# A routed two-expert decoder step on one core: the first two tiles take their slots from the position counts, and four pieces of the order move

## What is computed

```python
h = x @ w_in                      # 1024 -> 2048: values, two gates, conv input
y = concat(pool_out, conv_out) @ w_out
x = layer_norm(ALPHA * x + y)
# top-1 group of 4, then top-2 of its 8 experts
g_top, g_idx = top_k(softmax(x @ w_group + b_group), 1)
e_top, e_idx = top_k(softmax(e_logits_of_that_group), 2)
gate = g_top * e_top / sum(e_top)
for e in range(32):
    hdn = silu(x @ w1[e]) * (x @ w3[e])     # 1024 -> 512
    acc += combine[:, e] * (hdn @ w2[e])    # 512 -> 1024
out = layer_norm(ALPHA * x + acc)
```

## Time and profile before

| what | value |
|---|---|
| median of 3 runs | 716.95 us (716.07 to 717.56) |
| the profiled execution | 716.73 us |
| its span | 715.0 us |
| PE busy (matmul) | 609.8 us, 85% |
| DVE, ACT, POOL busy | 306.9, 181.8, 158.4 us |
| moved by the DMA queues | 235.99 MB, mean 330 GB/s |
| of it weights of the experts | 96 loads of 2048 KB |

### The profile page before, as it was taken

How to read it: one execution, slowest core, us unless ns; L and a number is a source line. 1 busy time by engine, 2 the same in 40 slices (tenths; PEclk the granted TensorE clock), 3 DMA queues, 4 the chain that set the end, 5 groups by cost and what they waited for, 6 DMA issues and landing times.

```text
span 715.0 us, 10596 instructions
## 1 busy us (share of the span) xinstructions
PE 609.8 (85%) x4220; PEld 420.6 (59%) x4220; DVE 306.9 (43%) x787; ACT 181.8 (25%) x287; POOL 158.4 (22%) x181
## 2 busy tenths in 40 slices
PE   5999999999999999889877987988788777877771
PEld 5999999878775556446444544554344435453440
DVE  4462485517577133353442353342434251433244
ACT  3323313302111313223232323322232121223130
POOL 1000000000000414244235224332341322233142
PEclk9999999999989999999999999899999999999996
DMA  9952133834496999999999999999999999999950
GB/s 250 282 184 90 45 118 105 339 135 190 152 392 250 390 418 420 417 416 417 422 416 421 413 422 416 422 416 421 422 418 421 415 422 420 425 415 418 404 223 21
DMA packets 45738, 235.99 MB, mean 330 GB/s; under 512 B 13667, under 2 KB 18275, under 8 KB 28712
## 3 DMA queue, kind: packets, MB, share of 16 engines
q1 hardware_dynamic: 32287, 220.92, 76.6%
q0 software_dynamic: 12544, 11.71, 4.9%
q10 hardware_dynamic: 857, 2.67, 0.9%
HBM read 237.69 MB, written 30.20 MB: 375 GB/s over the span
## 4 chain that ended last, share of the span: by engine, by line
PE 34%; issue 19%; DMA 17%; SPq 15%; POOL 9%; DVE 5%; ACT 1%; POOLq 0%; DVEq 0%; ACTq 0%
PE ps L534 14%; SPq L402 9%; PE ps L591 7%; DMA tenth_block<-in_w 6%; DMA blocks<-in_w 6%; PE ps L694 6%; SPq L406 5%; PE ps L715 2%; POOL out L1085 2%; POOL out L1081 2%; POOL prev L1077 2%; POOL first_outputs L1073 2%; DMA first_outputs<-ye,first_row 2%; DMA x_tok<-in_x_prompt 1%; DMA prev<-first_outputs,final_row 1%
## 5 line engine op out<-in xcount | busy, mean ns | idle before, releaser
L694 PE MATMUL ps<-blocks,ln 128*64 128x256 f32 x1952 | 233.5, 396 | 53.6 <-DMA blocks<-in_w 32.4
L694 PEld LDWEIGHTS ps<-blocks,ln 128*64 128x64 f32 x1952 | 157.0, 143 | 130.2 <-issue 57.2
L715 PE MATMUL ps<-blocks,hT 128*64 128x512 f32 x464 | 105.7, 596 | 6.0 <-DMA blocks<-in_w 5.8
L1077 POOL DMA_INDIRECT prev<-first_outputs,final_row x32 | 34.9, 1091 | 246.7 <-DMA first_outputs<-ye_more,first_row 119.3
L715 PEld LDWEIGHTS ps<-blocks,hT 128*64 128x64 f32 x464 | 32.8, 137 | 59.8 <-issue 48.5
L798 ACT ACTIVATE ln<-ps 128x512 f32<-128x512 f32 (+1 forms) x38 | 19.9, 572 | 112.2 <-PE ps L682 89.0
L1494 DVE SCALAR_TENSOR_TENSOR h_rows<-silu,slot_gate,ps 128x256 f32<-128x256 f32 x33 | 15.7, 477 | 69.0 <-PE ps L694 68.9
L1499 DVE COPY hT<-ps 128x256 f32<-128x256 f32 x33 | 13.9, 422 | 71.1 <-PE ps L703 71.1
L534 PE MATMUL ps<-xT_high,w_in_high 128*128 128x288 f32 x256 | 41.4, 305 | 0.9 <-DVE xT_low L1187 0.9
L981 ACT ACTIVATE std<-rstd,eps 128x1 f32<-128x1 f32 x32 | 9.4, 295 | 125.3 <-DVEq L1523 125.2
L534 PE MATMUL ps<-xT_low,w_in_high 128*128 128x288 f32 x256 | 39.5, 297 | 0.0
(11 more groups left out here) (232 smaller groups left out, 789.6 us busy)
## 6 DMA issues: line engine op xcount, KB each, us to landing
blocks<-in_w SPq DMA_DIRECT2D x87, 2048.0 KB, 36.5
tenth_block<-in_w SPq DMA_DIRECT2D x9, 2048.0 KB, 37.9
blocks<-in_w_in SPq DMA_DIRECT2D x3, 2048.0 KB, 10.5
blocks<-in_w_out SPq DMA_DIRECT2D x2, 2048.0 KB, 7.8
x_tok<-in_x_prompt SPq DMA_DIRECT2D x4, 512.0 KB, 5.2
blocks<-in_w_in SPq DMA_DIRECT2D x4, 512.0 KB, 11.3
first_outputs<-in_x_prompt SPq DMA_DIRECT2D x4, 512.0 KB, 8.7
x_rows<-x_tok ACTq DMA_DIRECT2D x4, 512.0 KB, 2.7
```

The lines of the kernel that those rows point to most:

```text
L694: mm = pe.matmul(ps[64 * g:64 * g + 64, bank, 0:FH], x, w[:, k, g * FH:(g + 1) * FH], start=(k == 0), stop=(k == KD - 1))
L715: mm = pe.matmul(ps[64 * g:64 * g + 64, BY, :], hT[:, k % 2, k // 2 * SLOTS:(k // 2 + 1) * SLOTS], w[:, k, g * DH:(g + 1) * DH], start=(k ...
L1077: return g.indirect_dma_start(out=prev[w], out_offset=None, in_=first_rows[:, :], in_offset=rows_at(idx), bounds_check=last_row, oob_is_er ...
```

## The change

- **Head.** `project(0)`'s first half no longer waits for the low part of the weights before its first 16 matmuls, only before the last 8; the turn of tile 3 moves behind this first half.
- **Mask.** VectorE makes `mask` from the chosen group and experts directly, before `picked`, and the two differences for the gates behind it. The position and count matmuls take 64 rows instead of 128 for the last tile.
- **Slots of tiles 0 and 1.** `hot_first` comes from two small operations on the position counts of experts 0 and 1 and two comparisons, in place of the matching over all ten choices. It stands before the sums for the table.
- **First pair.** TensorE's order after tile 0's w3 becomes: gather of tile 1, table matmuls, turn of tile 1, tile 1's w1, turn of tile 0's hidden, tile 1's w3, down of tile 0. ScalarE copies tile 1's rows before it waits for the table.
- **End.** The last w2 is loaded in two halves with a semaphore each, and `down` waits for the second one midway. VectorE does `final(31)` before `products(32)`, and the last tile's sum in two parts: the filled row first, the product when it comes; POOL issues `store(31)` ahead of `load(31)`, and `load(31)` ahead of `send(30)`. The stores count on two semaphores by even and odd tile.

The diff, cut to its core (the semaphores' declarations, and the loop for further tiles, which does not run here, are left out):

```diff
@@ -454,7 +455,12 @@
             def load(n):
                 kind, t = LOADS[n]
-                if kind == "w2":
+                if kind == "w2" and t == E:
+                    e = expert_of(t)
+                    src = w2[bass.DynSlice(e, 1)].rearrange("e f d -> (e f) d").rearrange("(g p c) d -> p g c d", g=2, c=KF // 2)
+                    for g, landed in ((0, block_loaded[HOME[n]]), (1, last_loaded)):
+                        sp.dma_start(out_block(HOME[n])[:, 2 * g:2 * g + 2, :], src[:, g, :, :]).then_inc(landed, 16)
+                elif kind == "w2":
                     load_out(HOME[n], expert_of(t))
...
@@ -500,7 +506,7 @@
                     mm.then_inc(x_turned, 1)
 
-            for j in range(4):
+            for j in range(3):
                 turn_x(j)
...
@@ -519,17 +525,20 @@
 
                 part, g = c // NG, c % NG
-                pe.wait_ge(w_low, c + 1)
+                pe.wait_ge(w_high, c + 1)
                 if c in (2, 3) or 4 <= c < 10:
                     pe.wait_ge(in_act, c - 1)
                 elif c >= 10:
                     pe.wait_ge(in_dve, c - 9)
                 for h in range(2):
                     if c == 0 and h:
+                        turn_x(3)
                         turn_x(4)
                     if c == 0:
                         pe.wait_ge(xT_low, (6, 2 * NT)[h])
                     for i, (a, b) in enumerate(((0, 0), (0, 1), (1, 0))):
+                        if a:
+                            pe.wait_ge(w_low, c + 1)
                         for k in range(KD):
...
@@ -703,14 +711,14 @@
                 mm.then_inc(h_turned, 1)
 
-            def down(b, loads, seq, halfway=None):
+            def down(b, loads, seq, last=False):
                 w = out_block(b)
                 pe.wait_ge(block_loaded[b], loads)
                 wait(pe, y_kept, seq)
                 pe.wait_ge(hT_ready, seq + 1)
                 for k in range(KF):
-                    if halfway and k == KF // 2:
-                        halfway()
+                    if last and k == KF // 2:
+                        pe.wait_ge(last_loaded, 16)
                     for g in range(2):
...
@@ -723,13 +731,14 @@
                 into_hidden("w1", 0, 16, 0, 0)
                 into_hidden("w3", 1, 16, 0, 0)
+                fetch_first(1)
                 token_table()
-                fetch_first(1, lambda: turn_hidden(0))
-                down(2, 16, 0, lambda: turn_first(1))
+                turn_first(1)
                 pe.wait_ge(xeT_ready, 2)
                 into_hidden("w1", 3, 16, 1, 1)
+                turn_hidden(0)
                 into_hidden("w3", 4, 16, 1, 1)
-                pe.wait_ge(table_ready, 1)
+                down(2, 16, 0)
                 turn_hidden(1)
...
@@ -751,7 +760,7 @@
                 into_hidden("w3", *place("w3", E), E, 0)
                 turn_hidden(E)
-                down(*place("w2", E), E)
+                down(*place("w2", E), E, last=True)
 
...
@@ -999,11 +1008,11 @@
             keep_xeT_first(0)
             silu_of(0)
-            act.wait_ge(table_ready, 1)
             keep_xe_first(1)
-            fill_second()
             keep_xeT_first(1)
             silu_of(1)
+            act.wait_ge(table_ready, 1)
+            fill_second()
             keep_xeT(1)
...
@@ -1097,11 +1106,12 @@
             def store(t):
                 pool.wait_ge(y_kept, t + 1)
-                store_first(t % YR, first_row[:, t:t + 1]).then_inc(first_stored, 16)
+                store_first(t % YR, first_row[:, t:t + 1]).then_inc(more_first if t == E else first_stored[t % 2], 16)
 
             def load(t):
+
                 w = (t - 1) % ZR
-                pool.wait_ge(first_stored, 16 * t)
+                pool.wait_ge(first_stored[(t - 1) % 2], 16 * ((t - 1) // 2 + 1))
                 wait(pool, final_stored[w], 32 * ((t - 1) // ZR))
...
@@ -1126,12 +1136,17 @@
             store(1)
             load(2)
-            for t in range(2, E):
+            for t in range(2, E - 1):
                 store(t)
                 send(t - 1)
-                load(t + 1)
+                if t < E - 2:
+                    load(t + 1)
                 if t % 2 == 0 and t // 2 + 2 <= PAIRS:
                     fetch(t // 2 + 2)
+            store(E - 1)
+            load(E - 1)
+            send(E - 2)
+            load(E)
             send(E - 1)
...
@@ -1354,7 +1369,6 @@
             gmax, m1, m2, ex = [top[:, i, :] for i in range(4)]
             choose(EG, lg, gmax, g_hot, g_tmp)
-            v.tensor_tensor(g_tmp, lg, gmax.unsqueeze(2).to_broadcast([P, NT, EG]), ALU.subtract).then_inc(diff_ready, 1)
 
...
@@ -1363,6 +1377,11 @@
             settled(v.scalar_tensor_tensor(e_val, e_hot[:, :, 0, :], -3.0e38, e_val, ALU.mult, ALU.add))
             choose(EPG, e_val, m2, e_hot[:, :, 1, :], e_tmp)
+            settled(v.tensor_tensor(e_tmp, e_hot[:, :, 0, :], e_hot[:, :, 1, :], ALU.add))
+            v.tensor_tensor(mask.rearrange("p n (g e) -> p n g e", g=EG),
+                            g_hot.unsqueeze(3).to_broadcast([P, NT, EG, EPG]),
+                            e_tmp.unsqueeze(2).to_broadcast([P, NT, EG, EPG]), ALU.mult).then_inc(mask_ready, 1)
+            v.tensor_tensor(g_tmp, lg, gmax.unsqueeze(2).to_broadcast([P, NT, EG]), ALU.subtract).then_inc(diff_ready, 1)
             v.tensor_tensor(m2, m2, m1, ALU.subtract).then_inc(diff_ready, 1)
...
@@ -1370,8 +1389,6 @@
             settled(last)
             settled(v.memset(picked[64:P, NT - 1, :, :], 0.0))
-            v.tensor_tensor(mask, picked[:, :, 0, :], picked[:, :, 1, :], ALU.add).then_inc(mask_ready, 1)
-
 
...
@@ -1380,42 +1397,22 @@
                 return x.unsqueeze(1).to_broadcast([P, n, x.shape[-1]])
 
+            dve.wait_ge(pos_done, 1)
+            pos_of = ps[:, 5, 0:NT * E].rearrange("p (n e) -> p n e", n=NT)
+            slot_of = first_slot[:, :].rearrange("p (i n) -> p i n", i=2)
+            for i in range(2):
+                last = v.scalar_tensor_tensor(slot_of[:, i, :], pos_of[:, :, i], 1.0, mask[:, :, i], ALU.add, ALU.mult)
+            settled(last)
+            settled(v.tensor_scalar(first_slot[:, :], first_slot[:, :], -1.0, None, ALU.add))
+            for i in range(2):
+                v.tensor_tensor(hot_first[:, i, :, :], iota[:, :].unsqueeze(1).to_broadcast([P, NT, SLOTS]),
+                                slot_of[:, i, :].unsqueeze(2).to_broadcast([P, NT, SLOTS]), ALU.is_equal).then_inc(hot_ready, 1)
+
             settled(v.tensor_tensor(prod, pick, row(iota[:, 0:E], A), ALU.mult))
             settled(v.tensor_reduce(expert, prod, AX.X, ALU.add))
             dve.wait_ge(tail_stored, 64)
-            dve.wait_ge(pos_done, 1)
-            settled(v.tensor_tensor(product, picked, ps[:, 5, 0:NT * E].rearrange("p (n e) -> p n e", n=NT)
-                                    .unsqueeze(2).to_broadcast([P, NT, 2, E]), ALU.mult))
+            settled(v.tensor_tensor(product, picked, pos_of.unsqueeze(2).to_broadcast([P, NT, 2, E]), ALU.mult))
             settled(v.tensor_reduce(pos, prod, AX.X, ALU.add))
-
-            settled(v.tensor_scalar(col, pos, float(SLOTS), 1.0e6, ALU.is_ge, ALU.mult))
-            settled(v.scalar_tensor_tensor(base, expert, float(SLOTS), pos, ALU.mult, ALU.add))
-            settled(v.tensor_tensor(rel[:, :], base, col, ALU.add))
-
-            def match_slots(n):
-
-                wait(dve, hot_ready, n)
-                wait(dve, rel_moved, n)
-                v.tensor_tensor(equal[:, :, :], iota[:, :].unsqueeze(1).to_broadcast([P, A, SLOTS]),
-                                rel[:, :].unsqueeze(2).to_broadcast([P, A, SLOTS]), ALU.is_equal).then_inc(matched, 1)
-
-            both = equal[:, :, :].rearrange("p (n k) c -> p n k c", k=2)
-
-            def sum_choices(n, into):
-                dve.wait_ge(matched, n + 1)
-                v.tensor_tensor(into, both[:, :, 0, :], both[:, :, 1, :], ALU.add).then_inc(hot_ready, 1)
-
-            def move_rel(n):
-
-                dve.wait_ge(matched, n + 1)
-                v.tensor_scalar(rel[:, :], rel[:, :], -float(SLOTS), None, ALU.add).then_inc(rel_moved, 1)
-
-            match_slots(0)
-            move_rel(0)
-            sum_choices(0, hot_first[:, 0, :, :])
-            match_slots(1)
-            sum_choices(1, hot_first[:, 1, :, :])
-
 
...
@@ -1507,10 +1504,13 @@
 
             def finish(t, u, w, in_order):
-
                 dve.wait_ge(y_kept, t + 1)
                 in_order(v.tensor_tensor(prev[w], prev[w], ye[u], ALU.add))
                 dve.sem_inc(prev_added, 1)
+                norm2(t, w, in_order)
+
+            def norm2(t, w, in_order):
+
                 in_order(v.bn_stats(stats[:, 0, :], prev[w]))
...
@@ -1532,6 +1532,18 @@
                     dve.wait_ge(ln2_loaded, 64)
                 finish(t, t % YR, w, settled)
+
+            def last_final():
+
+                u, w = E % YR, (E - 1) % ZR
+                dve.wait_ge(prev_loaded[w], 16 * ((E - 1) // ZR + 1))
```

(14 more changed lines are left out.)

28 lines of the change are left out of this document (14 added, 14 removed).

## The result

| | before | after |
|---|---|---|
| median | 717.25 us (716.07 to 718.53) | 726.44 us (724.48 to 730.07, 4 runs) |
| ratio, 95% interval | | 1.0127 [1.0092, 1.0162] |
| profiled execution, span | 716.73, 715.0 | 724.48, 722.7 |

The changed kernel is 1.3% slower, and the interval is clear of 1. Its profiled execution is the fastest of its four. I compare the two traces first, and come back to the other 2 us of the median at the end.

What follows compares the result with a forecast made beforehand. The DMA queues' stream of expert weights (413 to 425 GB/s from 250 to 661 us) sets the end, not TensorE. Forecast 716.73 - 2.3 (head) + 5.5 (refill, slots included) + 4.7 (end) = 724.6 us, range 718.0 to 729.0.

Steps and rivals of the forecast that it cites:

- Head, -2.3: First products: clock stays up, second half product starts at 18.5 instead of 20.86 us, a gain of 2.3 us.
- the other end that the prediction gave, -0.6: Head: if the clock falls as before, the first half costs 1.7 us more and only -0.6 is left.
- this shift is carried to the release of the early blocks: Head: TensorE works almost without a gap to 160 us, so the -2.3 reaches the early blocks' release.
- Slots, -0.6: Routing: tile 0's gather starts at 208.16 instead of 208.76, behind keep_warm; only 0.6 of some 2.2 us arrives.
- the 64-row matmuls cost and save nothing: Routing: taking 64 rows for the last tile's position and count matmuls changes the time by nothing.
- Refill, +5.5: First pair: load 12 at 243.1 instead of 237.03, queue idle 13.3 instead of 7.8 us; +5.5, slots' 0.6 included.
- the stall before pair 1: Refill: TensorE stands idle for the turn of pair 1, worth nothing while the queue holds three blocks.
- End, +4.7: After the last landing: products(32) waits behind final(31), +2.7, and TensorE's low clock costs 2.0 more.
- Rival A: Stream makes the refill gap up, so late load 12 costs nothing; 714.6 or 717.7 us; chance 0.12.
- Rival B: End pays: load(31) lands before 690.6, two-part sum saves 1.4, total 718.5 us; chance 0.16.
- Rival C: Slow side: head's clock falls (-0.6) and load(31) lands late (+6.5), total 728.1 us; chance 0.12.
- D: Rival that changes don't do what they say; already forecast in the slots, where keep_warm takes most; no chance of its own.

Runs made afterwards that it cites:

- e1: Changed kernel with TensorE's old order of the first pair and tile 0's sum ahead of tile 1's products; 721.44 us.
- e2: Changed kernel with the old end (VectorE's order, one sum, POOL's order, last w2 in one piece); 722.64 us.
- e3: Changed kernel with old first pair and old end, leaving the new head, early mask and slots from counts; 717.69 us, ratio 1.0009.
- e5: Kernel before with the new head alone; 716.14 us, ratio 1.0000.
- e10: e9 with 14 instead of 21 keep_warm matmuls ahead of the position matmuls; 714.53 us, ratio 0.9969.
- e6: Changed kernel with tile 0's hidden turn and down directly behind the turn of tile 1, ahead of tile 1's w1; 725.59 us, ratio 1.0116.
- e8: e3 with the two-part sum and the last w2 in halves kept, products and copy of tile 32 ahead of final(31); 717.49 us, ratio 1.0007.
- e9: e3 with 2 instead of 12 keep_warm matmuls behind the position matmuls; 716.39 us, ratio 0.9992.
- e7: Changed kernel with VectorE's copy of tile 0's hidden turn moved behind the release of the table; 726.92 us, ratio 1.0127.
- e11: Changed kernel with the table matmuls ahead of the gather of tile 1, tile 0's down still last; 728.06 us, ratio 1.0153.
- e4: Kernel before with final(31) moved ahead of products(32) on VectorE, nothing else; 723.02 us, ratio 1.0080.
- e12: e9 with the old head; 716.85 us, ratio 0.9996.

## Why the prediction was right, and where it was off

- **The forecast** was 724.6; the profiled execution took 724.48, the median 726.44. The range (718.0 to 729.0) holds both, and the sign and the two causes are as argued. The closeness of the first is luck: the runs spread over 5.6 us, and two errors cancel. Up to the last `w3` the sum has +3.2 and the traces +2.3; behind it the sum has +4.7 and the traces +5.4.
- **Head, -2.3.** The second half product came at 17.53, a microsecond sooner than the 18.5 given, and then lost it to the clock, whose fall I had looked for in the first half only. At the release -1.8 was left. Where the clock stayed up (e1, e2, e3, e5, e10) the second half starts at 17.9 to 18.3 and -2.4 to -2.6 arrives, as forecast; where it fell in the first half (e6, e8, e9), at 19.4 to 19.7 and -1.1 to -1.5 arrives, toward the other end that the prediction gave, -0.6; in e7 and e11 the half starts later still and nothing arrives. I had taken one of two cases for the rule: the clock stayed up in five of eleven traces of the new head. The step that failed is the next one: "this shift is carried to the release of the early blocks" is true, but the sum went on as if it were carried to the end. In medians the head, mask and slots together, -2.3 - 0.6 by my terms, gave +0.4 (e3, not to be told from 0). Behind the release stands a stretch at 1.2 GHz whose length has two values 3.4 us apart, and I had priced the `keep_warm` there by one trace of the shorter kind.
- **Slots, -0.6.** "Twelve more `keep_warm` matmuls hold TensorE" is right: the gather starts right behind them. But only 0.28 of the 0.6 arrived, since "the 64-row matmuls cost and save nothing" is wrong: from the first position matmul to `keep_warm` it is 0.87 us (202.95 to 203.82) instead of 0.50 (204.74 to 205.24). With the long low stretch, e5 against e3, it was 0.1. What I passed over is that this is no reason to price it low and go on, but the fault to be mended (e9, e10).
- **Refill, +5.5** (of which +6.1 the order of the pair). The mechanism stands in the steps that the traces show. From tile 0's `w3` (load 10) to load 12 I had 243.1 - 222.0 = 21.1, measured 20.51. The copy in the midst of the table work, the stall before pair 1 (3.47) and the empty windows are there. The gap's cost was 4.8 in queue idle against before (4.6 and 4.7 for the order of the pair alone, after against e1 and e2 against e3), 5.0 in the medians: inside the range given (3.8 to 7.0), a microsecond under the value. The sum of idle shares over small transfers was the uncertain part and remained it.
- **End, +4.7.** Measured 29.1 - 23.65 = 5.4 in the trace, 3.8 to 5.8 in the medians. Two rows carry the difference: `load(31)` landed 7.0 after its issue, not 6.4 (e4, with POOL's old order: 6.4, 688.81 to 695.24); the hidden turn took 0.70 at the low clock instead of 0.50. `down` at half pace cost 2.0, as written.
- **Rival A** (0.12) falls by the table of eleven traces. **Rival B** (0.16), that the end pays: no, its condition failed. `final(31)` began at 697.75, when the last `w3` was already done (693.62 + 3.67 = 697.29), because its load was issued at 690.69 only. No run met the condition, so the 1.4 us of B was not tested; e8 shows only that the two-part sum and the halves of w2 win 0.1 us or less where `final(31)` comes behind `products`. **Rival C** (0.12), the slow side, was half true: the median lies between forecast and C. Its fall of the clock came, in this trace in the second half product, in e6, e8, e9 and e11 in the first; its late load did not (7.0 us to landing, +5.4 in place of +6.5). **D**, that `keep_warm` eats the slots' gain, was in the forecast and held. The 2 us between the profiled execution and the median fit a longer low stretch (1.6 in the routing, or one more in the head). The mean granted clock falls as the runs get longer, 0.962, 0.959, 0.957 and 0.943 for 724.48, 725.42, 727.46 and 730.07 us, but the three other runs have no trace, so where it fell is not shown.

## What to carry to other kernels

When a queue sets the pace, count only what the queue stands idle: here one constant plus the release and that idle gave the start of the last `w3` within 0.8 us in fourteen kernels. An engine that does several chains in order has several gates of almost the same height, so move a step only after asking what stands behind it on each engine (here `down`, the table, and the copy between them: 20.5 and 19.7 us behind load 10). And when a result becomes ready sooner, look for the filler work that was sized for the old moment: 17 `keep_warm` matmuls fewer were worth 3.2 us by medians (e3 717.69, e10 714.53), the new head alone at most 1.3. And take more than one trace before you price a stretch in which the clock falls: here the same instructions gave 0, 3.4 or 6.8 us of low clock in the head.

## What the runs showed of the hardware

- The low-clock stretch behind the routing logits was 6.8 or 10.2 us long in fourteen traces, never anything between, with the same instructions (e1 and e3). In all of them TensorE had an idle time of 1.38 us, then small matmuls, near the point where the clock fell (between 0.2 us before and 2.3 after the end of that idle time).
- In the head the new order had 0, 3.4 or 6.8 us at the low clock (eleven traces: 5, 5 and 1), and the release moved with it from 186.40 to 189.77.
- Ten `keep_warm` matmuls fewer before a dense gather did not lower the clock in it: 4.51 us for its 20 matmuls with 12 of them (after, before) or with 2 (e9, e10, e12).
- POOL's load of tile 31 took 7.0 us from issue to landing with the store of tile 31 issued ahead of it (after), 6.4 with it behind (before, e4); e1, with it ahead, has 7.0 again. It is a small cost of the new order by itself.
- From the first position matmul to the next `keep_warm` it took 0.87 us with 64 rows for the last tile (after, e3), 0.50 with 128 (before, e5).
